# A hybrid decoder step on Trainium2: RMSNorm rows turned by a product with a diagonal, their norm weight applied by GpSimd, TensorE given idle products first

## What is computed

```python
def rmsnorm(x, w):
    xf = x.astype(jnp.float32)
    y = xf * lax.rsqrt(jnp.mean(xf * xf, axis=-1, keepdims=True) + NORM_EPS)
    return (y * w.astype(jnp.float32)).astype(x.dtype)
...
for i in range(DEPTH):
    up = rmsnorm(hp, norm_pre[i])
    ...  # yp = mixer(up) @ w_out
    hp = hp + rmsnorm(yp, norm_post[i])
```

## Time and profile before

| | |
|---|---|
| median of 3 runs | 1395.72 us (1395.53 to 1396.22) |
| the profiled execution, its own time | 1389.81 us |
| its span, first to last instruction | 1388.0 us |
| PE busy | 1308.3 us, 94% |
| DVE, ACT, POOL busy | 796.8, 628.4, 473.3 us |
| mean granted TensorE clock | 0.982 |

### The profile page before, as it was taken

One profiled execution on the slowest core, in us unless ns is written; L12 is line 12 of the kernel. 1 busy time (PEld: TensorE's weight loads), 2 busy tenths in 40 slices (PEclk: granted clock), 3 DMA queues, 4 the chain that ended last, 5 costly groups with the idle time before them and its releaser, 6 DMA issues. The chain is left out here.

```text
span 1388.0 us, 30371 instructions
## 1 busy us (share of the span) xinstructions
PE 1308.3 (94%) x11346; PEld 1255.7 (90%) x11346; DVE 796.8 (57%) x1525; ACT 628.4 (45%) x1409; POOL 473.3 (34%) x399
## 2 busy tenths in 40 slices
PE   5999999999999999999998988699998999999996
PEld 4999999999899999999998988598897988979995
DVE  4444455453555534654444144677979969697544
ACT  4333333333324334334343244457667765765432
POOL 0545423554224553235522212002424443262011
PEclk9999999999999999999999999699999999999998
DMA  6574442753335634367422252354463735644251
GB/s 189 147 205 120 103 108 85 207 145 92 107 85 172 189 94 108 85 179 229 113 81 73 86 166 59 110 149 128 115 191 92 207 116 158 196 145 117 77 171 65
DMA packets 313416, 182.63 MB, mean 132 GB/s; under 512 B 75233, under 2 KB 302257, under 8 KB 312881
## 3 DMA queue, kind: packets, MB, share of 16 engines
q1 hardware_dynamic: 313264, 180.64, 45.7%
HBM read 155.01 MB, written 46.41 MB: 145 GB/s over the span
## 5 line engine op out<-in xcount | busy, mean ns | idle before, releaser
L1418 POOL TENSOR_TENSOR wlo<-w,whi 128x1024 fp32r<-128x1024 f32 x95 | 227.9, 2399 | 461.6 <-ACT whi L1060 461.6
L897 PE MATMUL at_proj<-uhi,whi 128*128 128x272 f32 x1536 | 336.1, 300 | 5.9 <-POOL wlo L1418 2.8
L897 PE MATMUL at_proj<-uhi,wlo 128*128 128x272 f32 x1536 | 320.1, 290 | 0.0
L897 PE MATMUL at_proj<-ulo,whi 128*128 128x272 f32 x1536 | 319.2, 290 | 0.0
L1060 ACT ACTIVATE whi<-w 128x1024 fp32r<-128x1024 f32 x95 | 100.7, 1059 | 339.8 <-PE at_proj L897 309.4
L897 PEld LDWEIGHTS at_proj<-uhi,whi 128*128 128x128 f32 x1536 | 241.6, 191 | 9.3 <-issue 5.1
L897 PEld LDWEIGHTS at_proj<-ulo,whi 128*128 128x128 f32 x1536 | 243.8, 190 | 0.0
L897 PEld LDWEIGHTS at_proj<-uhi,wlo 128*128 128x128 f32 x1536 | 242.3, 191 | 0.0
L1893 PE MATMUL sd_proj<-uhi,whi 128*128 128x272 f32 x768 | 168.0, 300 | 4.7 <-DVEq L2306 2.2
L1893 PE MATMUL sd_proj<-ulo,whi 128*128 128x272 f32 x768 | 159.4, 289 | 0.0
L1893 PE MATMUL sd_proj<-uhi,wlo 128*128 128x272 f32 x768 | 159.3, 289 | 0.0
(11 more groups left out here) (307 smaller groups left out, 2276.9 us busy)
## 6 DMA issues: line engine op xcount, KB each, us to landing
w<-in_attn_w_in_dram SPq DMA_DIRECT2D x88, 512.0 KB, 4.3
w<-in_ssd_w_in_dram SPq DMA_DIRECT2D x40, 512.0 KB, 4.2
w<-in_attn_w_out_dram SPq DMA_DIRECT2D x16, 512.0 KB, 4.0
sd_h<-in_state_ssm_dram SPq DMA_DIRECT2D x16, 512.0 KB, 6.5
sd_bc<-acs_p SPq DMA_DIRECT2D x16, 512.0 KB, 5.2
out_s_ssm_dram<-sd_h SPq DMA_DIRECT2D x16, 512.0 KB, 3.5
w<-in_ssd_w_out_dram SPq DMA_DIRECT2D x16, 512.0 KB, 4.0
at_k_cache<-in_cache_kv_w_dram SPq DMA_DIRECT2D x384, 16.0 KB, 2.7
```

The source lines that it names most:

```text
L897: last = pe.matmul(proj[:, r, h, 0:HALF], a[:, r, kk * P:(kk + 1) * P], b[:, kk, h * HALF:(h + 1) * HALF], start=(kk == 0 and a is whi and ...
L1418: pool.tensor_tensor(wlo[:, r], w[:, r], whi[:, r].bitcast(F32), ALU.subtract).then_inc(wlo_ready, 1)
```

## The change

It touches only `mix_phase`, and acts only where `pre` is given, so in m1.

- `normed` (L524) is gone from DVE. POOL forms `weighed = xt * w_pre` for each tile as soon as h is there, into two buffers; from the third tile on it waits until tile i-2 has been turned.
- ACT, after the root of tile i, forms a 128x128 diagonal `diag` from the identity and the inverse roots; it first waits for its own root.
- PE turns by a plain product: `acc = weighed^T diag`, stationary `weighed`, moving `diag`, in place of the transpose. That scales and turns at once. It waits for `weighed` and for `diag`.
- PE runs 28 products of the identity by the identity ahead of the first tile, right after the last `turn`, and two before each later tile, in a PSUM tile that is free.

```diff
-        normed = m.sb("normed", [P, 2, D])
+        weighed = m.sb("weighed", [P, 2, D])
+        diag = m.sb("diag", [P, 2, P])
...
             turn(KD - 1)
+
+            def keep_warm(n):
+
+                for _ in range(n):
+                    pe.matmul(back[:, 0, 0, 0:P], ident[:, :], ident[:, :], start=True, stop=True)
+
             if pre is not None:
+                pe.wait_ge(rows_ready, KD - 1)
+                keep_warm(28)
                 for i in range(TT):
-                    pe.wait_ge(normed_ready, i + 1)
+                    if i:
+                        keep_warm(2)
+                    pe.wait_ge(weighed_ready, i + 1)
+                    pe.wait_ge(diag_ready, i + 1)
                     if i >= 2:
                         pe.wait_ge(lo_ready, i - 1)
                     r = ROWS[i]
                     for k in range(KD):
-                        last = pe.transpose(acc[:, i % 2, k // 4, (k % 4) * r:(k % 4 + 1) * r],
-                                            normed[0:r, i % 2, k * P:(k + 1) * P], ident[0:r, 0:r])
+                        last = pe.matmul(acc[:, i % 2, k // 4, (k % 4) * r:(k % 4 + 1) * r],
+                                         weighed[0:r, i % 2, k * P:(k + 1) * P], diag[0:r, i % 2, 0:r],
+                                         start=True, stop=True)
                     last.then_inc(turned_ready, 1)
...
                     act.activation(stats[0:n, 5, i:i + 1], stats[0:n, 4, i:i + 1], ACT.Sqrt).then_inc(rstd_ready, 1)
+                    act.wait_ge(rstd_ready, i + 2)
+                    if i >= 2:
+                        act.wait_ge(turned_ready, i - 1)
+                    act.activation(diag[0:n, i % 2, 0:n], ident[0:n, 0:n], ACT.Copy, scale=stats[0:n, 5, i:i + 1]) \
+                        .then_inc(diag_ready, 1)
...
-                if 2 <= step <= TT + 1:
-                    i, n = step - 2, ROWS[step - 2]
-                    dve.wait_ge(rstd_ready, i + 2)
-                    if i == 0:
-                        dve.wait_ge(pre_in, 16)
-                    if i >= 2:
-                        dve.wait_ge(turned_ready, i - 1)
-                    dve.scalar_tensor_tensor(out=normed[0:n, i % 2, :], in0=xt[0:n, i, :], scalar=stats[0:n, 5, i:i + 1],
-                                             in1=w_pre[0:n, :], op0=ALU.mult, op1=ALU.mult).then_inc(normed_ready, 1)
...
+            if pre is not None:
+                pool.wait_ge(pre_in, 16)
+                for i, n in enumerate(ROWS):
+                    pool.wait_ge(h_ready, i + 1)
+                    if i >= 2:
+                        pool.wait_ge(turned_ready, i - 1)
+                    pool.tensor_tensor(weighed[0:n, i % 2, :], xt[0:n, i, :], w_pre[0:n, :], ALU.mult) \
+                        .then_inc(weighed_ready, 1)
```

More of the change, by code:

```diff
@@ L314, in mix_phase @@
         h_ready, h_squares, stored = m.sem("h_ready"), m.sem("h_squares"), m.sem("stored")
-        normed_ready, turned_ready, hi_ready, lo_ready = \
-            (m.sem(n) for n in ("normed_ready", "turned_ready", "hi_ready", "lo_ready"))
+        weighed_ready, diag_ready, turned_ready, hi_ready, lo_ready = \
+            (m.sem(n) for n in ("weighed_ready", "diag_ready", "turned_ready", "hi_ready", "lo_ready"))
         block = ctx.enter_context(nc.Block())
```

## The result

The changed kernel takes 1397.93 us (median of 9 runs, 1397.32 to 1401.27); the kernel before, timed beside it, 1395.33 us (median of 9, 1392.52 to 1396.22). The ratio is 1.0029, 95% interval 1.0018 to 1.0039: 4.0 us slower, 2.5 to 5.4. The forecast was 3.5 us more and 1399.2 us. By the bound of 0.2% this is slower, though only just: the interval begins at 0.18%.

A forecast was written before the change was run, and what follows sets the result against it. PE, busy 1308 of 1388 us, was taken to bound the kernel, with the tail following a chain across engines. Tail +3.7 less 0.16 after it gave +3.5 us on the 1395.7 median: 1399.2 us, range 1394.8 to 1402.0.

The forecast's parts named there:

- What leaves DVE: Tail of the first mix phase: five DVE instructions of 1.27 us go, 6.3 us of 19.65 busy, no saving by itself.
- What POOL does to DVE: Tail: POOL's product and DVE's h block each other, taking 2.26 us for POOL and 1.14 for DVE per turn.
- The sum: Tail chain: last h ends at 882.6, 9.6 us more to the end, 892.2 instead of 888.47, +3.7 us.
- PE's new work: Tail on PE: two passes per product, a group of eight 1.95 us, 28 idle products 7 us, costing nothing.
- After the tail: Start of SSD: at full clock PE arrives 1.9 us earlier but waits 1.9 longer for loads; 0.16 us counted as gain.
- POOL goes twice: Rival, tail: POOL's second product goes ahead of DVE's third h; +5.4 - 0.16, 1401.0 us; chance 0.20.
- No meeting: Rival, tail: h and POOL's product run side by side, not slower; -0.5 - 0.16, 1395.0 us; chance 0.20.
- The clock falls anyway: Rival, tail: PE idles and drops to half clock, group 3.9 us; 1402.2 us, or +1 us if partly; chance 0.13.

The follow-up runs named there:

- e4_dve_weighs: Changed kernel with the product by the norm weight on DVE instead of POOL, POOL idle in the tail; tail 23.10 us, profiled execution 1401.28 us.
- e1_no_pool: Changed kernel without POOL's product by the norm weight, PE turning x itself; tail 20.55 us (changed kernel 24.48), profiled execution 1395.91 us.
- e2_pool_writes: Changed kernel with POOL only filling its tile with ones (memset) instead of multiplying; tail 20.54 us, profiled execution 1394.78 us.
- e6_order: Changed kernel with ACT's copy of a high part moved ahead of the square of the same step; tail 19.93 us, profiled execution 1395.01 us.
- e12_warm_no_gate: Kernel before with idle products throughout the tail (28, 8 ahead of each later group, 8 behind the last); tail 20.62 us, offset 10.08, profiled execution 1393.14 us.
- e3_no_idle: Changed kernel without any idle product (the 28 and the pairs); tail 24.50 us against 24.48, profiled execution 1396.93 us.
- e9: Kernel before with ACT's high part ahead of the square, idle products throughout the tail, own semaphore for the first time-step load; median 1393.02 us, ratio 0.9984.
- e11: Changed kernel with ACT's high part ahead of the square, own semaphore for the first time-step load, four idle products behind the last group; median 1393.53 us, ratio 0.9985.
- e10_order_warm: Kernel before with ACT's high part ahead of the square and idle products throughout the tail, no added semaphore; tail 18.42 us, median 1393.66 us, ratio 0.9989.

## Why the prediction was right, and where it was not

**What leaves DVE.** Right that the 6.3 us (5.9 measured) are no saving by themselves. Without POOL's part they are worth 2.55 us (e4_dve_weighs against e1_no_pool), and the diagonals and double passes that replace them take 2.22 of it back.

**What POOL does to DVE.** Right, and the main term. The third h was to end 5.88 us after the start of the first one and ended 5.77 after (875.69); the fourth was foreseen at 9.28 and came at 9.07; the last at 15.0 and came at 14.66. In each the blocked instruction ended at the end of the other plus its own time less 0.1 to 0.2 us, as in the earlier trace rows. e2_pool_writes shows that POOL's reading is needed for it: a POOL instruction that only writes delays nothing.

**The sum.** Tail +3.7 forecast, +3.60 measured. The lag of the last h was a little too large (0.3 us), and the stretch behind it a little too small: 9.6 forecast, 9.82 measured (884.58 to 894.40), where the diagonal takes 0.40 us, not the 0.29 to 0.3 of the row I took it from. The two errors cancel for the most part, which is luck. The sentence that named ACT's square, root and diagonal ahead of the first high part carried more than I gave it: e6_order shows that in this kernel the delay goes through it, and that behind it POOL's chain waits as the next bound.

**PE's new work.** Two passes a product, right: a group of eight is 2.05 us (forecast 1.95), the block of 28 takes 6.42 (7). The Trainium skill ("TensorE: Matmul & The Clock Gate", Terms) states that transpose mode is four times as fast for FP32, from which the forecast had the estimate of 3.6 us for a group. The traces do not agree: at full clock a group is 2.05 us against 1.09 for eight transposes (e12_warm_no_gate), a factor of 1.9 for this shape.

**After the tail.** Here the step failed. The clock was not at 1.00 through the tail: PE had stood still from 880.5 to 883.0; the clock was then at half from 883.4 to 886.6, and again from 893.6 to 900.4, 6.8 us of which the last 5 lie in SSD. There was no faster PE, and no wait of 2 us before the product of the time step; the offset grew by 0.21 instead of shrinking by 0.16. That an early PE would for the most part only have waited was right, but is shown by e12_warm_no_gate (1.4 us more of waiting for 1.7 us less of PE busy), not by the changed kernel. That the time came out all the same is partly luck: a group took 3.42 us where I had 1.95, but the engines behind it had not been ready for it, as e3_no_idle shows, in which PE's lower clock costs nothing.

**The rivals.** *POOL goes twice* did not happen: at the first meetings the two alternate, as the forecast had it. The Trainium skill ("SBUF — State Buffer", Who interferes with whom) says that the one that issued first goes first, and the trace agrees: DVE is ready for the third h at 872.69, POOL for its second product only when its first ends at 874.65, and the h is next. POOL's third and fourth do follow one another, but in a time when DVE asks for nothing, as the sum had it. *No meeting* is refuted by the h of 3.00 us; what it would have given for the tail, -0.5 us by my sum, is near what e1_no_pool and e2_pool_writes have (-0.33 and -0.34). *The clock falls anyway* happened in part, and its price was wrong: I had 1 us for a part and 3 us for all of it; e3_no_idle shows a tail at a mean clock of 0.71 that is no longer at all. The range, 1394.8 to 1402.0, held the result (its ends are 0.2 us below the two rivals' sums, 1395.0 and 1402.2, that they stand for), and slower by over 0.2% had the largest chance.

What stays open: why e4_dve_weighs took 1401.28 us in its one run, which of e9 and e11 is faster, what the tail would be with the new order and DVE's products away but not on POOL, and why DVE and POOL take turns here while at 1034.84 DVE waited through three POOL instructions.

## What to carry to other kernels

Work that is taken off the busiest engine of a stretch is worth less than its busy time as long as another engine's program order decides when results move on. Here 5.6 us less on DVE were worth 2.55, and what had to be put in their place cost 2.22 of that. Moving one copy ahead of one square gave 0.9 us in the old kernel and 4.6 in the new, and only then did an engine's work set the tail: DVE's in e10_order_warm, POOL's with its waits in e6_order. So mend the order first, then move the work. Before work goes to POOL, look whether DVE reads two SBUF tensors at that time, and find what stands in order behind the instruction that will be late. Idle products helped SSD here only where they ran up to the meeting of the engines (and in e10_order_warm not even then), and they must not be last at the meeting point. A faster PE needs its loads earlier as well.

## What the runs showed of the hardware that I had not expected

- In the changed kernel's tail DVE and POOL exclude each other and take turns, between two engines that each have their next instruction waiting: POOL 3.3 us, h 3.0 us, with handovers that save 0.1 to 0.2 us. A POOL memset of the same 128x1024 block takes 0.95 us and neither waits nor makes h wait.
- A group of eight transposes of 32 rows (32x32 output) costs PE 0.68 us at full clock (1.09 with 128 rows), and eight plain products of the same shape 1.97 us, nearly that of 128 columns (2.05): the plain product gains almost nothing from a small tile.
- Without idle products the clock did come back inside the changed kernel's tail (e3_no_idle, mean 0.71), while in the kernel before it stayed at 0.50 to the end. PE was busy for 13.73 of 24.50 us in the one and 8.94 of 20.88 in the other.
